# Nine gate blocks moved behind the last convolution tile, its normalised rows passed through three engines in lagged steps, and the sums of the spatial gate's layer norm made on GpSimd

## The reference, cut to what matters

```python
# first block: the spatial gate, beside a long convolution (hyena)
z = h @ w_in + b_in                      # z_u, z_v (1024 each), z_h (3072), z_g (4096)
vn = layer_norm(gelu(z_v), ln_g, ln_b)   # mean and variance over 1024 columns
mixed = einsum('gqp,bnpgc->bnqgc', w_s, vn) + b_s
y_a = (gelu(z_u) * mixed) @ w_branch_a

# second block: the conformer convolution
u = h @ w_in                             # a, b, z, 2048 columns each
v = a * sigmoid(b)
v = depthwise_conv(v, dw, 31 taps) + dw_b
v = silu(layer_norm_2(v, ln_g, ln_b))    # mean and variance over 2048 columns
return (v * silu(z)) @ w_out
```

## Time and profile before

| what | value |
|---|---|
| median of 3 runs | 2718.67 us (2713.81 to 2718.98) |
| time of the profiled execution | 2711.61 us |
| its span, first to last instruction | 2709.8 us |
| mean granted TensorE clock | 0.98 of 2.4 GHz |
| TensorE busy with matmuls | 2555.0 us, 94% |
| VectorE, ScalarE, GpSimd busy | 2007.7, 1391.0 and 784.1 us (74%, 51%, 29%) |

### The profile page before, as it was taken

The page is one execution under the profiler, slowest core; times in us unless marked ns, Lnnn a source line. Parts: engine busy times, 40 slices in busy tenths (PEclk is TensorE's granted clock), DMA queues, the critical chain, the costliest instruction groups (busy, mean ns, idle before and its releaser), DMA issues.

```text
span 2709.8 us, 42774 instructions
## 1 busy us (share of the span) xinstructions
PE 2555.0 (94%) x16616; PEld 2321.8 (86%) x16616; DVE 2007.7 (74%) x2588; ACT 1391.0 (51%) x2177; POOL 784.1 (29%) x742
## 2 busy tenths in 40 slices
PE   4589998999998999999999989999799999999979
PEld 2478887888986888888888879999689999999978
DVE  7889765877888876555555668888767788888855
ACT  0154433444445544445544466667556667666653
POOL 0200000001225610001111229666103566666530
PEclk9899999999999999999999989999899999999989
DMA  8878755687774886555555534444354444444424
GB/s 318 328 269 277 248 203 169 222 284 244 272 271 152 285 278 239 192 187 185 188 194 190 190 110 156 164 148 156 126 177 162 143 156 149 154 151 152 150 100 153
DMA packets 146627, 534.61 MB, mean 197 GB/s; under 512 B 16663, under 2 KB 16824, under 8 KB 145976
## 3 DMA queue, kind: packets, MB, share of 16 engines
q1 hardware_dynamic: 143176, 520.33, 55.9%
q0 software_dynamic: 3248, 11.54, 1.3%
HBM read 525.51 MB, written 6.29 MB: 196 GB/s over the span
## 4 chain that ended last, share of the span: by engine, by line
PE 78%; DVE 10%; issue 5%; ACT 5%; DMA 2%; POOL 0%; SPq 0%; DVEq 0%; ACTq 0%; POOLq 0%
PE ps L549 33%; PE ps L553 23%; PE ps L551 7%; PE ps L552 7%; DVE wl L982 2%; DVE AF L1001 2%; PE ps L594 2%; ACT wh L1692 2%; PE ps L919 1%; PE ps L676 1%; PE ps L820 1%; PE ps L664 1%; DVE BF L1591 1%; DVE BF L1581 1%; PE ps L614 1%
## 5 line engine op out<-in xcount | busy, mean ns | idle before, releaser
L982 DVE TENSOR_TENSOR wl<-ring,wh 128x1024 fp32r<-128x1024 f32 x784 | 1028.8, 1325 | 389.0 <-ACT wh L1692 387.8
L553 PE MATMUL ps<-A,wl 128*128 128x256 f32 x4480 | 1266.5, 283 | 0.0
L1692 ACT CAST wh<-ring 128x1024 fp32r<-128x1024 f32 x784 | 813.4, 1044 | 380.0 <-PE ps L553 360.6
L553 PEld LDWEIGHTS ps<-A,wl 128*128 128x128 f32 x4480 | 857.9, 192 | 0.5
L549 PE MATMUL ps<-A,wh 128*128 128x512 f32 x2176 | 775.5, 401 | 18.4 <-DVE A L986 8.4
L551 PE MATMUL ps<-A,wh 128*128 128x256 f32 x2304 | 675.2, 293 | 15.3 <-DVE A L986 10.9
L549 PE MATMUL ps<-B,wh 128*128 128x512 f32 x1792 | 637.5, 401 | 26.5 <-DVE wl L982 8.9
L552 PE MATMUL ps<-A,wh 128*128 128x256 f32 x2304 | 654.6, 284 | 0.0
L549 PEld LDWEIGHTS ps<-A,wh 128*128 128x128 f32 x2176 | 412.1, 189 | 118.0 <-issue 14.2
L553 PE MATMUL ps<-B,wl 128*128 128x256 f32 x1792 | 503.3, 281 | 0.0
L551 PEld LDWEIGHTS ps<-A,wh 128*128 128x128 f32 x2304 | 444.1, 193 | 18.2 <-issue 11.4
(11 more groups left out here) (246 smaller groups left out, 2299.1 us busy)
## 6 DMA issues: line engine op xcount, KB each, us to landing
ring<-in_w_m SPq DMA_DIRECT2D x256, 512.0 KB, 4.5
ring<-in_hgrn_w_in SPq DMA_DIRECT2D x160, 512.0 KB, 3.7
ring<-in_w_ada SPq DMA_DIRECT2D x144, 512.0 KB, 6.7
ring<-in_w_in SPq DMA_DIRECT2D x144, 512.0 KB, 5.2
ring<-in_conv_w_in SPq DMA_DIRECT2D x96, 512.0 KB, 3.7
AF<-in_w_ada SPq DMA_DIRECT2D x48, 512.0 KB, 8.5
ring<-in_w_ab SPq DMA_DIRECT2D x32, 512.0 KB, 5.4
ring<-in_w_o SPq DMA_DIRECT2D x32, 512.0 KB, 5.4
```

The lines of the kernel that those rows point to most:

```text
L553: return e.matmul(dst[:, 0:256], lo, x[:, 0, :], start=False, stop=last)
L982: e.tensor_tensor(low[:], ring[SLOT[h]][:], hi[:].bitcast(F32), ALU.subtract).then_inc(s.lo, 1)
L1692: e.copy(wh[h % NSPLIT][:], ring[SLOT[h]][:]).then_inc(s.hi, 1)
```

## The change

In the spatial gate, GpSimd adds the v tiles (`sum_v`) and the squares (`sum_squares`) together and TensorE makes one row sum of each; the orders of ScalarE, VectorE and GpSimd around it are moved, and the whole gate stands four blocks later. In the convolution, seven z blocks in place of ten stand between the pairs and nine at the end; one tap of each tile moves from TensorE to ScalarE and GpSimd; `scale_rows` is spread over ticks 8 to 68; and the passage of the rows starts at tick `LAST_TILE` + 13 = 89 in steps of two rows, one step a tick (`norm_step`, `rows_of`): multiply in step s, Silu in s + 1, gate in s + 2, round in s + 3, rest in s + 4. The gated rows get eight buffers of their own, `gated_rows`.

```diff
-NZ = 10
+NZ = 7
-NPOOL = 12
-NPE = 4
+NPOOL = 13
+NPE = 3
+NORM_FROM = LAST_TILE + 13
+NORM_STEPS = 12
+def rows_of(step):
+    return range(max(2 * step, 0), min(2 * step + 2, 16))
+    v_sum, v_squares = misc[:, 2048:2304], misc[:, 2304:2560]
+    gated_rows = [misc[:, 256 * i:256 * i + 256] for i in range(8)]
 # TensorE
         def spatial():
-            for i in range(8):
-                w.wait_ge(s.vmu, 1)
-                w.wait_ge(s.vsq, i + 1)
-                row_sum(ps[3][:, 0:256], 1, sgu_sq[i % 2], i, 8, s.vss)
-                if i % 4 == 0:
-                    yield
-            yield
-            yield
-            yield
+            w.wait_ge(s.vsum, 7)
+            w.wait_ge(s.spec, 16)
+            row_sum(ps[3][:, 0:256], 1, v_sum, 0, 1, s.vmean)
+            for _ in range(5):
+                yield
+            w.wait_ge(s.vmu, 1)
+            w.wait_ge(s.vsum, 14)
+            row_sum(ps[3][:, 0:256], 1, v_squares, 0, 1, s.vss)
+            for _ in range(4):
+                yield
...
-                    if 34 <= i < 42:
-                        w.wait_ge(s.uv, i - 25)
-                        w.wait_ge(s.spec, 16)
-                        row_sum(ps[3][:, 0:256], 1, vv(i - 34), i - 34, 8, s.vmean)
 # VectorE
+        def norm_step(step):
+            for i in rows_of(step):
+                if i in (2, 6, 10):
+                    centre_rest((i + 2) // 4)
+                if i % 4 == 0:
+                    w.wait_ge(s.sub, 26 + i // 4 + 1)
+                e.tensor_tensor(BF[:, i, :], BF[:, i, :], rstd, ALU.mult).then_inc(s.nm, 1)
+            for i in rows_of(step - 2):
+                if i % 2 == 0:
+                    gate_z(i)
+            for i in rows_of(step - 4):
+                conv_low(i)
...
+            if tick >= NORM_FROM:
+                norm_step(tick - NORM_FROM)
...
-        for i in range(16):
-            normed(i)
+        for step in range(2 * len(N_CV) - NORM_FROM, NORM_STEPS):
+            norm_step(step)
 # ScalarE
             for g in range(8):
+                if g % 2 == 0:
+                    yield
                 w.wait_ge(s.vsub, g + 1)
-                w.wait_ge(s.vss, g - 1)
-                e.activation(sgu_sq[g % 2].rearrange("p (a b) -> p a b", a=1), vv(g).unsqueeze(1),
-                             ACT.Square).then_inc(s.vsq, 1)
+                w.wait_ge(s.vsum, 7 + g - 1 if g >= 2 else 0)
+                e.activation(sgu_sq[g % 2], vv(g), ACT.Square).then_inc(s.vsq, 1)
...
+        def norm_step(step):
+            for i in rows_of(step - 1):
+                w.wait_ge(s.nm, 32 + i + 1)
+                w.wait_ge(s.ss, 18 + 16)
+                if i >= 8:
+                    wait_lo(w, i - 8, 3)
+                e.activation(gated_rows[i % 8], BF[:, i, :], ACT.Silu, scale=col("conv_ln_g_2", i),
+                             bias=col("conv_ln_b_2", i)).then_inc(s.silu, 1)
+            for i in rows_of(step - 3):
+                wait_gated(w, i)
+                e.copy(Bl[:, i, :], gated_rows[i % 8]).then_inc(s.ahi, 1)
 # GpSimd
-        for m in range(7):
+        def sum_v(g):
+            w.wait_ge(s.uv, 9 + g)
+            ...
+            vsum.up(e.tensor_tensor(v_sum, vv(0) if g == 1 else v_sum, vv(g), ALU.add))
+        def sum_squares(g):
+            w.wait_ge(s.vsq, g + 1)
+            w.wait_ge(s.vsum, vsum.n)
+            vsum.up(e.tensor_tensor(v_squares, sgu_sq[0] if g == 1 else v_squares, sgu_sq[g % 2], ALU.add))
+        for m in range(5):
             spectrum(m)
+        for g in range(1, 4):
+            sum_v(g)
+        spectrum(5)
+        for g in range(4, 6):
+            sum_v(g)
+        spectrum(6)
+        for g in range(6, 8):
+            sum_v(g)
         group(0)
         spectrum(7)
+        group(1)
         for g in range(1, 8):
+            sum_squares(g)
+        for g in range(2, 8):
             group(g)
...
-            if 8 <= tick < 24:
-                scale_rows(tick - 8)
+            if tick % 4 == 0 and 8 <= tick < 72:
+                scale_rows(tick // 4 - 2)
```

More of the change, by code:

```diff
@@ L192 @@
     "tr ut fwd hv inv skip y "
-    "vmean vmu vsub vsq vss vn vt vtc vmx vad ug "
+    "vsum vmean vmu vsub vsq vss vn vt vtc vmx vad ug "
     "ablo gy mx gp "
@@ L1176, in spatial @@
                 e.tensor_tensor(vv(g).unsqueeze(1), vv(g).unsqueeze(1), bc, ALU.subtract).then_inc(s.vsub, 1)
-                if g % 4 == 0:
+                if g % 4 == 3:
                     yield
-            yield
+            for _ in range(5):
+                yield
             w.wait_ge(s.sd, 1)
@@ L1182, in spatial @@
             w.wait_ge(s.rc, 1)
-            w.wait_ge(s.vss, 8)
+            w.wait_ge(s.vsq, 8)
             for i in range(8):
@@ L1447, in gate_z @@
         def gate_z(i):
-            x = ptmp[i % NTMP]
+            x = gated_rows[i % 8]
             w.wait_ge(s.silu, i + 1)
@@ L1501, in conv_behind @@
                 e.reciprocal(rstd, rstd).then_inc(s.rc, 1)
+                w.wait_ge(s.rc, 5)
+            if tick >= NORM_FROM:
+                norm_step(tick - NORM_FROM)
         for i, n in enumerate(N_CV):
@@ L1768, in spatial @@
         def spatial():
-            w.wait_ge(s.vmean, 8)
+            w.wait_ge(s.vmean, 1)
             e.copy(statb[:, 0:256], ps[3][:, 0:256]).then_inc(s.vmu, 1)
             for g in range(8):
+                if g % 2 == 0:
+                    yield
                 w.wait_ge(s.vsub, g + 1)
-                w.wait_ge(s.vss, g - 1)
-                e.activation(sgu_sq[g % 2].rearrange("p (a b) -> p a b", a=1), vv(g).unsqueeze(1),
-                             ACT.Square).then_inc(s.vsq, 1)
-                if g % 4 == 0:
-                    yield
-            w.wait_ge(s.vss, 8)
+                w.wait_ge(s.vsum, 7 + g - 1 if g >= 2 else 0)
+                e.activation(sgu_sq[g % 2], vv(g), ACT.Square).then_inc(s.vsq, 1)
+            yield
+            yield
+            w.wait_ge(s.vss, 1)
             w.wait_ge(s.ones, 5)
@@ L1981, in tap_step @@
                     prod.up(e.activation(dst, cp[:, j:j + 256], ACT.Copy, scale=col("conv_dw_2", 16 * j + n)))
-        def high7(i):
-            wait_gated(w, i)
-            e.copy(Bl[:, i, :], ptmp[i % NTMP]).then_inc(s.ahi, 1)
-        def gated(i):
-            w.wait_ge(s.nm, 32 + i + 1)
-            w.wait_ge(s.padd, (NPOOL - 1) * 16)
-            if i >= NTMP:
-                wait_lo(w, i - NTMP, 3)
-            e.activation(ptmp[i % NTMP], BF[:, i, :], ACT.Silu, scale=col("conv_ln_g_2", i),
-                         bias=col("conv_ln_b_2", i)).then_inc(s.silu, 1)
-            if i >= 2:
-                high7(i - 2)
-            if i == 15:
-                high7(14)
-                high7(15)
+        def norm_step(step):
[9 more added lines that the diff above has]
+                e.copy(Bl[:, i, :], gated_rows[i % 8]).then_inc(s.ahi, 1)
         def square_step(n, step):
@@ L2044, in scalar_program @@
                 e.activation(BF[:, n - 16, :], BF[:, n - 16, :], ACT.Silu).then_inc(s.sgz, 1)
-        for i in range(16):
-            gated(i)
+        for step in range(2 * len(N_CV) - NORM_FROM, NORM_STEPS):
+            norm_step(step)
         def next_high(n):
@@ L2206, in group @@
             e.dma_start(bsb[g % 2], d["sgu_b"][g:g + 1, :].to_broadcast([P, P])).then_inc((s.ws0, s.ws1)[g % 2], 16)
-        for m in range(7):
-            spectrum(m)
+        vsum = Tally(s.vsum)
+        def sum_v(g):
+            w.wait_ge(s.uv, 9 + g)
+            w.wait_ge(s.vsum, vsum.n)
+            w.wait_ge(s.zh, 24)
+            vsum.up(e.tensor_tensor(v_sum, vv(0) if g == 1 else v_sum, vv(g), ALU.add))
+        def sum_squares(g):
+            w.wait_ge(s.vsq, g + 1)
+            w.wait_ge(s.vsum, vsum.n)
+            vsum.up(e.tensor_tensor(v_squares, sgu_sq[0] if g == 1 else v_squares, sgu_sq[g % 2], ALU.add))
+        for m in range(5):
+            spectrum(m)
+        for g in range(1, 4):
[6 more added lines that the diff above has]
+            sum_v(g)
         group(0)
         spectrum(7)
+        group(1)
         for g in range(1, 8):
+            sum_squares(g)
+        for g in range(2, 8):
             group(g)
@@ L2315, in gpsimd_program @@
                 w.wait_ge(s.sgz, silus(i))
-                e.tensor_tensor(ptmp[i % NTMP], ptmp[i % NTMP], BF[:, 16 + i, :], ALU.mult).then_inc(s.gzp, 1)
+                e.tensor_tensor(gated_rows[i % 8], gated_rows[i % 8], BF[:, 16 + i, :], ALU.mult).then_inc(s.gzp, 1)
             if i >= 2 and i % 3 == 0:
-                low_part(Bl[:, 16 + i - 2, :], ptmp[(i - 2) % NTMP], Bl[:, i - 2, :], s.ahi, 48 + i - 1, s.alo_p)
+                low_part(Bl[:, 16 + i - 2, :], gated_rows[(i - 2) % 8], Bl[:, i - 2, :], s.ahi, 48 + i - 1, s.alo_p)
         def head(hd):
```

17 lines of the change are left out of this document (1 added, 16 removed).

## The result

The changed kernel took 2696.95 us (median of four runs, 2694.76 to 2697.56) where the kernel before took 2718.82 (2713.81 to 2723.17): a ratio of 0.9912, 95% interval 0.9898 to 0.9926, 21.9 us faster. The forecast was 2683, so 14 us of the forecast gain of 36 did not come. The time lies 0.05 us inside the range for 8 in 10, 2673 to 2697, and outside the forecast's own range of 2676 to 2690.

A forecast was written before the change was run, and what follows sets the result against it. TensorE, busy 94% of the 2709.8 us span, was taken as the bound. Terms of -18, -6.5 and -9.5 sum to -34, taking the median to 2684.7; the forecast said 2683, range for 8 in 10 2673 to 2697.

The forecast's parts named there:

- Part 1: Spatial gate: fewer row sums on TensorE and less waiting there give -18 us, bounds -19.6 and -6.
- The 1.5 us that I took off for ScalarE standing at the squares: Spatial gate, block 43: allowance for ScalarE's squares waiting for GpSimd's sums and so delaying `hi`; 1.5 us.
- the margin: Spatial gate: `hi` and `lo` done after 13.3 us, TensorE arriving after 15.4 us; 2 us to spare.
- the gate's wait only moves: Rival at the spatial gate: TensorE waits for `hi` later instead, the gate gains only 6 to 8 us; 2696 us, chance 0.17.
- the one with loads: Rival at the spatial gate: the stretch is bound by loads, the gate gains only 3 us; 2700 us, chance 0.03.
- Part 2: Convolution's input product: one tap less per tile on TensorE gives -6.5 us, bounds -6.9 and -3.5.
- Spreading `scale_rows` costs nothing: Convolution: GpSimd's scalings keep their 13.8 us and are read only after the convolution; cost nothing.
- My new wait of VectorE's `cpad` operation for GpSimd: Convolution, two-block periods in a row: VectorE waits for GpSimd's additions, 1 to 2.5 us, twice.
- Part 3: Rows' passage after the convolution's input product: rows 8 to 15 begin at E + 15.8 instead of E + 25.3; -9.5 us.
- VectorE becomes the bound of the tail: Rival in the last blocks: VectorE's `lo` is late, E moves out, the passage gains only 2 us; 2692 us, chance 0.15.
- GpSimd as a bound that makes the kernel slower: Rival in the convolution: GpSimd's additions take 1.52 us instead of 1.02 and bound it; 2752 us, chance 0.03.
- The port: Shared VectorE and GpSimd port: 30 more additions at 0.5 us each could cost VectorE 15 us; the sum has 3.

The follow-up runs named there:

- e1: The kernel before with only the spatial gate's change to the sums, convolution and rows' passage as before: 2694.5 us, ratio 0.9921.
- e12: The changed kernel with the mean's eight row sums back on TensorE and no `sum_v` on GpSimd: 2699.6 us, ratio 0.9932.
- e6: The changed kernel with six gate blocks last instead of nine (NZ 10), the tap still off TensorE: 2691.8 us, ratio 0.9903.
- e11: The changed kernel with GpSimd's scalings behind its last tap addition, and ScalarE's Silu and Sigmoid behind the next half's `hi`: 2683.3 us, ratio 0.9871.
- e8: The changed kernel with six gate blocks last instead of nine and the fourth tap back on TensorE: 2698.6 us, ratio 0.9934.
- e5: The changed kernel with GpSimd's sixteen scalings of the rows moved behind its last tap addition: 2689.0 us, ratio 0.9895.

## Why the prediction was right in part and 14 us off

**Part 1 was right, and small by 3 us.** Forecast 18, measured 20.7 (e1: 20.9 by the medians), which is past its bound of 19.6. The cause, order rather than work, holds in the sizes. The mean's seven row sums saved are 2.8 us (e12), and seven of squares at the same price make 5.6 for both. TensorE waited 9.7 us at the gate before, and the mean clock of 0.91 over 40 us cost another 3.6. That is 18.9 us together; 1.8 stay open. The 17.2 us of the earlier trace rows were too many for the wait, since TensorE's own was 9.1, but the 13.7 for wait and clock together was near the 13.3. Whether the new places alone would have done it, with eight row sums of squares still on TensorE, was not run. The 1.5 us that I took off for ScalarE standing at the squares was not lost: the wait is there, 10.1 us at its longest, and the margin held. The rival "the gate's wait only moves" did not occur, nor did the one with loads.

**Part 2 failed, at its cover.** The tap's price was right: 6.65 us beside 6.9. The step that failed is "VectorE has 250 - 216.87 = 33 us free over this middle and runs three halves, 8.7 us, ahead. Cost at TensorE: nothing, up to 3 us if both covers fail". It cost 10.5: 7.7 us of waiting, and 304.15 - 7.70 - 293.61 = 2.8 us in which TensorE was busy for longer with the same work. The 3.4 us at the lower clock make 1.7 of these; 1.1 stay open.

Most of the 33 us was not free. The earlier trace rows say that nearly all of VectorE's idle time before `lo`, 40.7 of 41.4 us, is waiting for `hi`. Waits of the kernel before, then of e6, over the stretch:

```profile
ACT tmpA L2041 <- DVE tmpA L1521: 45.0, 15, 4.6
DVE wl L982 <- ACT wh L1692: 43.5, 40, 1.5
ACT wh L1692 <- PE ps L553: 32.5, 21, 2.7
ACT BF L2044 <- DVE BF L1523: 12.2, 5, 4.2
```

```profile
DVE wl L990 <- ACT wh L1701: 34.5, 30, 1.4
ACT wh L1701 <- PE ps L564: 13.5, 14, 1.7
```

That VectorE's busy time and this wait fill the stretch, 255.8 + 43.5 = 299.3 of 300.2 us before and 258.5 + 34.5 = 293.0 of 293.6 in e6, says nothing yet: in e6 it did the same work and sixteen more GpSimd additions beside it, and 9 us of the wait went. What counts is what the `hi` had stood behind. I followed each wait back on ScalarE to the last thing that ScalarE itself had waited for. Before, 29.3 of the 43.5 us (21 waits, nearly all of 1.42 us) lie behind a Sigmoid or Silu that waited for VectorE's own scaling, and in e6 it is 29.4 of 34.5. That part is a ring between the two engines, and it did not shrink. The other 14.2 us lie mostly behind TensorE or in ScalarE's queue; they are slack, and shrank to 5.1. Over the middle of 250 us the ring has 21.3 of the 33. I had priced these 1.42 us in part 3, three times, and left them out in part 2. In e11 the ring has 1.6 us left, and the stretch takes TensorE's own time with the same nine blocks last and the same thirteen additions.

"Spreading `scale_rows` costs nothing" holds in the old order, where e8 has the scalings spread and takes 300.6 us like the kernel before. In the new order having them in the stretch costs 4.3 us (e5), of which the squares L2013 carry 1.2, `cpad` 1.1 and a `lo` 1.2. My new wait of VectorE's `cpad` operation for GpSimd was the right place but a small symptom, 0.7 us once. The addition has a mean of 1063 ns, not near 1000.

Several reliefs each take a part of the input product's time: the scalings 4.3 us, the tap 9.0 (2.3 net of its 6.7 on TensorE), the blocks' order 10.5, ScalarE's order 6.4 on top of the scalings. They overlap and can't be added. The order of ScalarE without late scalings was not tried, so how much of its effect needs them stays open.

**Part 3 had the mechanism and was 2.4 us short.** Forecast E + 15.8, measured E + 18.2: 7.1 gained of 9.5. The variance's VectorE operation came 20.9 us before E, not 21.6; from it to rows 8 to 15 took 39.1 us where 37.4 were counted. VectorE was busy for 33.1 of 38.7 us there, as counted; the rest is three waits of 1.42 us for `hi` and ScalarE's last steps. Once the holes and most of these waits are gone (e11), it is E + 15.6. That the lag itself is worth nothing (e8) I had not said, and the sum had not needed it.

**The sum.** By stretches: -20.7 + 3.8 - 7.1, -23.9 before rounding, forecast -18 - 6.5 - 9.5 = -34. Of the 10 us between them part 2 is 10.3, part 3 is 2.4, and part 1 gives 2.7 back. The rest of the 14 is the 2 us between stretches and medians and the 1.7 us that I took to be more likely than the sum. That the time is still inside the range is luck: the range was widened to 2697 for rivals that did not occur, and one of these, "the gate's wait only moves" at 2696, has nearly the measured time with a mechanism that the traces exclude. In kind "VectorE becomes the bound of the tail" (2692) came nearest: right in the engine, wrong in the place, since the passage kept 7.1 us of its gain and the loss lay in the input product. GpSimd as a bound that makes the kernel slower was far off: TensorE's holes were 7.7 us.

**The port.** Sixteen more additions beside the same VectorE work (e8 to e6) raise VectorE's busy time from 255.57 to 258.48 us, 0.18 us an addition, and TensorE doesn't see it. GpSimd's additions themselves grow from a mean of 1053 to 1087 ns. The prediction had half a microsecond an addition as the rule's estimate. The Trainium skill, SBUF — State Buffer, section Who interferes with whom, says of the shared port pair that whichever of the two issues first holds it for the whole instruction and blocks the other. The traces fit that in kind: in the changed kernel's passage the multiplications and rests (L1472, L994) with no GpSimd instruction beside them take 0.41 to 0.42 us, and the nine that take 0.6 to 0.96 all have one. In size the 15 us for thirty additions, each blocking one operation, would be 5.4 by the measured 0.18.

## What to carry to other kernels

Before idle time of an engine is spent as cover, look at what ends it, and then at what that instruction had waited for. If it stood behind the bounding engine, the wait is slack, and goes when that engine gets faster (14.2 us before, 5.1 in e6). If it stood behind something that waited for the idle engine's own work, it is a ring between the two, and counts as load (29.3 us before, 29.4 in e6). Then look at the order on the other engine: moving the activation that waits behind the instruction that is awaited cost nothing here, and took 9.2 us from input product and passage together (e5 to e11), where the late scalings took 4.1, six blocks last 2.0 and the tap back 1.5. And where an engine stands at many small sums in turn, the order of what they wait for counts first: of 20.7 us at the gate, fourteen row sums fewer were some 5.6.

## What the runs showed that was not expected

Each relief was forecast as a few microseconds and the effects are far from additive: thirteen additions cost nothing at 2.6 blocks a tile and 10.5 us at 2.4. Behind two holes of 1.5 and 2.4 us, six us apart, the granted clock was 0.88 and 0.95 on the mean of the two 10 us windows from 1860: 3.4 us at 1.2 GHz, which cost 1.7 us beside the 7.7 of waiting. A row sum that waited 2.6 us at 1756 was not followed by a lower clock. The same code from the last sum over weight chunks to the first tap product took 571.7 to 578.2 us, a scatter as large as most effects here, which is why two stretches of each profile told more than the medians.
